# First layer of a three-layer token mixer: two projection tiles fed side by side, weight leads one tile ahead, one root a tile later

## What is computed

```python
def hybrid_layer(h, hc, c_act, cc_act, norm_g, w_mod, b_mod, w_in, ...):
    shift, scale, gate = jnp.split((c_act @ w_mod + b_mod)[:, None, :], 3, axis=-1)
    shift_c, scale_c, gate_c = jnp.split(cc_act @ w_mod + b_mod, 3, axis=-1)
    lat = split_cols((rms_norm(h, norm_g) * (1.0 + scale) + shift) @ w_in)
    cx = split_cols((rms_norm(hc, norm_g) * (1.0 + scale_c) + shift_c) @ w_in)
    att_l, att_c = gqa_branch(...)      # attention
    hg_l, hg_c = hgrn_branch(...)       # gated linear recurrence, per-head norm behind it
    y_conv, y_four, g_att, g_hg = mix_stream(lat, conv_w)   # convolution and Fourier mixing
    y = jnp.concatenate([y_conv, att_l * g_att, hg_l * g_hg, y_four], axis=-1) @ w_out
    h_new = h + gate * y
    ...

def first_block(...):
    for layer in range(DEPTH):          # DEPTH = 2
        h, hc = hybrid_layer(h, hc, ...)
    return rms_norm(h, final_g)
```

## Time and profile before

| | us |
|---|---|
| median of 3 runs | 1932.18 |
| lowest and highest | 1930.01, 1933.41 |
| the profiled execution | 1931.5 |
| its span | 1929.7 |
| TensorE busy | 1747.3 (91%) |
| VectorE busy | 824.2 (43%) |
| ScalarE busy | 716.7 (37%) |
| GpSimd busy | 601.3 (31%) |
| mean granted clock of TensorE, share of full | 0.963 |

### The profile page before, as it was taken

The page is one execution under the profiler, slowest core; times in us unless marked ns, Lnnn a source line. Parts: engine busy times, 40 slices in busy tenths (PEclk is TensorE's granted clock), DMA queues, the critical chain, the costliest instruction groups (busy, mean ns, idle before and its releaser), DMA issues.

```text
span 1929.7 us, 32336 instructions
## 1 busy us (share of the span) xinstructions
PE 1747.3 (91%) x13588; PEld 1403.6 (73%) x13588; DVE 824.2 (43%) x1489; ACT 716.7 (37%) x1111; POOL 601.3 (31%) x318
## 2 busy tenths in 40 slices
PE   6799899978989988889889988888899899999996
PEld 2687788855878766667777757886578588888885
DVE  0301165447250255476547658655415433333112
ACT  3323413235342624354543965003434432222222
POOL 0121312183223323452024303212234234444442
PEclk9899999989999999999899999899999999999998
DMA  8344311130122211302432210000220223323231
GB/s 329 106 155 142 112 35 46 46 109 1 55 90 74 66 56 56 131 1 95 135 99 87 77 44 2 3 3 22 66 85 25 66 78 97 98 90 97 98 109 66
DMA packets 42569, 152.17 MB, mean 79 GB/s; under 512 B 4416, under 2 KB 5568, under 8 KB 42176
## 3 DMA queue, kind: packets, MB, share of 16 engines
q1 hardware_dynamic: 38880, 140.72, 22.1%
q10 hardware_dynamic: 3552, 9.44, 1.3%
HBM read 145.95 MB, written 4.19 MB: 78 GB/s over the span
## 4 chain that ended last, share of the span: by engine, by line
PE 41%; DVE 7%; ACT 2%; issue 2%; DVEq 0%; ACTq 0%
PE wide_ps L1770 29%; PE wide_ps L1791 2%; PE pair_ps L2344 1%; PE wide_ps L2341 1%; PE wide_ps L2320 1%; PE wide_ps L2279 1%; DVE xn L1688 1%; DVE xn L1538 1%; PE duo_ps L2448 1%; PE wide_ps L2429 1%; DVE h L1692 1%; PE wide_ps L1806 1%; DVE ring_r L1182 1%; PE pair_ps L2279 0%; DVE work L1598 0%
## 5 line engine op out<-in xcount | busy, mean ns | idle before, releaser
L534 POOL TENSOR_TENSOR ring_r<-ring,scratch_r 128x1024 fp32r<-128x1024 f32 x179 | 433.1, 2420 | 1075.9 <-ACT scratch_r L706 1047.8
L1770 PE MATMUL wide_ps<-xn_r,scratch_r 128*128 128x512 f32 (+1 forms) x1320 | 490.1, 371 | 0.0
L1770 PE MATMUL wide_ps<-work_r,scratch_r 128*128 128x512 f32 (+1 forms) x1151 | 445.9, 387 | 23.3 <-DVE xn_r L1174 12.4
L706 ACT ACTIVATE scratch_r<-ring 128x1024 fp32r<-128x1024 f32 x195 | 206.7, 1061 | 599.8 <-PE wide_ps L1770 457.4
L1770 PE MATMUL wide_ps<-work_r,ring_r 128*128 128x512 f32 (+1 forms) x1151 | 429.2, 373 | 0.0
L1770 PEld LDWEIGHTS wide_ps<-xn_r,scratch_r 128*128 128x128 f32 x1320 | 252.1, 191 | 49.3 <-issue 5.7
L1770 PEld LDWEIGHTS wide_ps<-work_r,scratch_r 128*128 128x128 f32 x1151 | 218.7, 190 | 75.7 <-issue 19.1
L1770 PEld LDWEIGHTS wide_ps<-work_r,ring_r 128*128 128x128 f32 x1151 | 218.9, 190 | 40.0
L1770 PE MATMUL wide_ps<-proj_r,scratch_r 128*128 128x512 f32 x704 | 238.1, 386 | 1.6 <-DVE proj_r L1174 1.6
L1770 PEld LDWEIGHTS wide_ps<-proj_r,scratch_r 128*128 128x128 f32 x704 | 132.8, 189 | 31.6 <-DVE proj_r L1174 2.5
L693 ACT ACTIVATE proj<-wide_ps 128x512 f32<-128x512 f32 (+2 forms) x116 | 73.9, 637 | 164.4 <-PE wide_ps L1770 154.8
(11 more groups left out here) (406 smaller groups left out, 2913.6 us busy)
## 6 DMA issues: line engine op xcount, KB each, us to landing
ring<-weights SPq DMA_DIRECT2D x256, 512.0 KB, 3.5
h<-tokens SPq DMA_DIRECT2D x4, 768.0 KB, 11.6
h<-tokens ACTq DMA_DIRECT2D x1, 3072.0 KB, 10.2
out<-h ACTq DMA_DIRECT2D x1, 2048.0 KB, 7.3
h<-out ACTq DMA_DIRECT2D x1, 2048.0 KB, 10.7
out<-h SPq DMA_DIRECT2D x8, 256.0 KB, 2.0
const_sb<-const SPq DMA_DIRECT2D x1, 1089.0 KB, 6.1
h<-mem ACTq DMA_DIRECT2D x1, 1024.0 KB, 13.2
```

The source lines that it names most:

```text
L534: pool.tensor_tensor(as_r(wt), wt, as_r(w_lead(m)).bitcast(F32), ALU.subtract).then_inc(w_split, 1)
L706: act.activation(as_r(w_lead(m)), ring[:, c % RING, :], ACT.Copy).then_inc(w_lead_ready, 1)
L1770: last = pe.matmul(wide_ps[:, bank, a:b], wt[:, cols], as_r(x[:, a:b]), start=n == 0 and p == 0, stop=n == len(k_order) - 1 and p == 2)
```

## The change

In layer 0:

- The stream's order puts the four late chunks of tiles 0 and 1 first, and then the chunks of tiles 0 and 1.
- PE does the parts of both tiles, with the turn of the first row between them, and then `project_two` for tiles 0 and 1; tile 2 uses `project_ahead`. Both as layer 1 has it already.
- Leads 0 and 1 lie in spots of their own. ACT makes lead 0 before `modulate`, and lead 1 inside it, before k = 1, with a row copy before each; after that step t makes lead t + 1 (where it made t + 2), and step 15 makes 16 and 17.
- POOL waits at tile 2 for the last `x_split`, as in layer 1.

In both layers:

- For odd k ACT, not DVE, casts the lead of the input (`mod_lead`); DVE only subtracts.
- `head_root(ly, 0)` is asked for in ACT's step 24, where it was 23, so behind the evacuation of tile 23.

```diff
@@ -71,9 +71,9 @@
 
 
     if stage == "late":
-        return PLAN["proj0"] + 3 * (n // 2) + n % 2
+        return PLAN["proj0"] + (n if n < 4 else 3 * (n // 2) + n % 2)
     if stage == "proj0":
-        return PLAN["proj0"] + (3 * n + 2 if n < MIXED else 2 * MIXED + n)
+        return PLAN["proj0"] + (4 + n if n < 2 else 3 * n + 2 if n < MIXED else 2 * MIXED + n)
     return PLAN[stage] + n
 
 
@@ -236,6 +236,7 @@
         w_lead_ready, w_split = sem("w_lead_ready"), sem("w_split")
         lead_ready = sem("lead_ready")
         x_lead, x_split = sem("x_lead"), sem("x_split")
+        mod_lead = sem("mod_lead")
         norm_lead = sem("norm_lead")
         mix_split_lead, mix_split = sem("mix_split_lead"), sem("mix_split")
         final_ready = sem("final_ready")
@@ -324,7 +325,7 @@
                     conv_tmp[:, :], qe_2[:, :])[k]
 
 
-        LEAD_SPOTS = {SPLIT_AT[name] + n: (name, n) for name in ("proj1", "ab_2", "cq", "gu") for n in range(2)}
+        LEAD_SPOTS = {SPLIT_AT[name] + n: (name, n) for name in ("proj0", "proj1", "ab_2", "cq", "gu") for n in range(2)}
         X_SPLITS = {"proj0": 0, "out0": KT, "proj1": KT + 1, "out1": 2 * KT + 1, "ck": 2 * KT + 2, "ab_2": 3 * KT + 2,
                     "out_2": 4 * KT + 2, "cq": 4 * KT + 6, "gu": 5 * KT + 6, "down": 6 * KT + 6}
         MIX_ORDER = [0, 1, 4, 5, 6, 7, 2, 3]
@@ -352,7 +353,7 @@
 
             if m not in LEAD_SPOTS:
                 return scratch[:, CHUNK * (m % 2):CHUNK * (m % 2 + 1)]
-            spot_at = {"proj1": 4 * TOK, "ab_2": 22 * LAT + N_CONST2 + 2 * KT * CTX + 4 * LAT, "cq": 22 * LAT + N_CONST2 + 2 * KT * CTX,
+            spot_at = {"proj0": 4 * TOK, "proj1": 4 * TOK, "ab_2": 22 * LAT + N_CONST2 + 2 * KT * CTX + 4 * LAT, "cq": 22 * LAT + N_CONST2 + 2 * KT * CTX,
                        "gu": 22 * LAT + N_CONST2 + 2 * KT * CTX}[LEAD_SPOTS[m][0]] + CHUNK * LEAD_SPOTS[m][1]
             return flat[:, spot_at:spot_at + CHUNK]
 
@@ -528,7 +529,7 @@
                 for n in chunks or range(SPLIT_CHUNKS[stage]):
                     c, m = where(stage, n), SPLIT_AT[stage] + n
                     pool.wait_ge(w_lead_ready, m + 1)
-                    if n == 2 and stage in ("proj1", "cq", "gu"):
+                    if n == 2 and stage in ("proj0", "proj1", "cq", "gu"):
                         pool.wait_ge(x_split, X_SPLITS[stage] + KT)
                     wt = ring[:, c % RING, :]
                     pool.tensor_tensor(as_r(wt), wt, as_r(w_lead(m)).bitcast(F32), ALU.subtract).then_inc(w_split, 1)
@@ -719,10 +720,16 @@
 
                 act.wait_ge(mod_ready, (2, 4)[ly])
                 for k in range(KT):
+                    if ly == 0 and k == 1:
+                        modulation_row(KT + 1)
+                        weight_leads("proj0", 1)
                     act.wait_ge(scaled, 8 * ly + k + 1)
                     for s, (a, b) in enumerate(pieces(TOK)):
                         act.activation(xn_t[:, k, a:b], xn_t[:, k, a:b], ACT.Identity, bias=mod[:, ly, k, s:s + 1],
                                        scale=mod_scale[:, ly, k, s:s + 1]).then_inc(xn_ready, 1)
+                    if k % 2:
+                        act.wait_ge(xn_ready, 16 * ly + 2 * k + 2)
+                        act.activation(as_r(lead_tile(k)), xn_t[:, k, :], ACT.Copy).then_inc(mod_lead, 1)
 
             def lower_bounds():
 
@@ -802,7 +809,7 @@
                 if t == 22:
                     values_by_token(ly, 1)
                     head_square(ly, 0)
-                if t == 23:
+                if t == 24:
                     head_root(ly, 0)
                 if t == 25:
                     for d in range(2):
@@ -917,13 +924,16 @@
                         act.wait_ge(tokens_landed[k // 2], 16)
                         square(0, k, h[:, k, :], TOK)
                     mean_root(0, TOK)
-                    weight_leads("proj0", 0, 2)
+                    weight_leads("proj0", 0)
+                    modulation_row(KT)
                 modulate(ly)
                 for t in range(NPROJ):
-                    if ly == 0 and t < MIXED:
+                    if ly == 0 and 2 <= t < MIXED:
                         modulation_row(KT + t)
                     recurrent_steps(ly, t)
-                    if t < LATE:
+                    if ly == 0 and 1 <= t < LATE:
+                        weight_leads("proj0", t + 1, 2 if t == LATE - 1 else 1)
+                    elif ly and t < LATE:
                         leads_after(f"proj{ly}", t)
                     evacuate(f"proj{ly}", t, where(f"proj{ly}", t) + 1, width(ly, t), proj[:, t, 0:width(ly, t)],
                              other(ACT.Silu) if t in SILU_TILES else ACT.Copy, bank=None if t < LATE else 0)
@@ -1380,7 +1390,12 @@
                         dve.tensor_tensor(xn_t[:, k, :], h[:, k, :], root[:, :], ALU.mult).then_inc(scaled, 1)
                     if k:
                         dve.wait_ge(xn_ready, 16 * ly + 2 * k)
-                        split(xn_t[:, k - 1, :], lead_tile(k - 1))
+                        if k % 2:
+                            split(xn_t[:, k - 1, :], lead_tile(k - 1))
+                        else:
+                            dve.wait_ge(mod_lead, KT // 2 * ly + k // 2)
+                            dve.tensor_tensor(as_r(xn_t[:, k - 1, :]), xn_t[:, k - 1, :], as_r(lead_tile(k - 1)).bitcast(F32),
+                                              ALU.subtract).then_inc(x_split, 1)
                 queries_keys(ly)
                 dve.wait_ge(conv_out, 2 * ly)
                 link(dve.memset(proj[:, CV, :], 0.0))
@@ -1779,7 +1794,8 @@
                 banks = []
                 for stage, tile in (first, second):
                     g, m = EVAC[stage] + tile, SPLIT_AT[stage] + tile
-                    pe.wait_ge(evacuated, g - 1)
+                    if g >= 2:
+                        pe.wait_ge(evacuated, g - 1)
                     pe.wait_ge(w_split, m + 1)
                     banks.append((wide_ps[:, g % 2, :], as_r(w_lead(m)), as_r(ring[:, where(stage, tile) % RING, :])))
                 for k in range(KT):
@@ -2110,22 +2126,23 @@
             norm_step(0, KT - 1, TOK)
             for ly in range(DEPTH):
                 for t in range(NPROJ):
-                    if ly == 0 and 0 < t <= MIXED:
+                    if ly == 0 and 1 < t <= MIXED:
                         modulation_turn(KT + t - 1)
                     if ly == 0 and t == 0:
                         pe.wait_ge(mod_ready, 1)
                     if ly == 0 and t < MIXED:
+                        if t == 1:
+                            modulation_turn(KT)
                         for half in range(2):
                             modulation_part(MOD_BLOCKS[KT + t][0], 2 * MOD_BLOCKS[KT + t][1] + half)
                     query_key_sums(ly, t)
                     normed = lambda k: xn_t[:, k, :]
-                    if ly and t == 0:
-                        project_two(("proj1", 0), ("proj1", 1), lead_tile, normed, TOK, after(X_SPLITS["proj1"]))
-                    elif ly and t == 2:
-                        project_ahead("proj1", 2, lead_tile, normed, width(ly, 2))
-                    elif ly == 0 or t > 2:
-                        project_split(f"proj{ly}", t, range(KT), lead_tile, normed, width(ly, t),
-                                      after(X_SPLITS["proj0"]) if t == 0 else None,
+                    if t == 1:
+                        project_two((f"proj{ly}", 0), (f"proj{ly}", 1), lead_tile, normed, TOK, after(X_SPLITS[f"proj{ly}"]))
+                    elif t == 2:
+                        project_ahead(f"proj{ly}", 2, lead_tile, normed, width(ly, 2))
+                    elif t > 2:
+                        project_split(f"proj{ly}", t, range(KT), lead_tile, normed, width(ly, t), None,
                                       (lambda n: recurrent_piece(ly, KT * (t - LATE) + n)) if t >= LATE else None)
                 pe.wait_ge(hg_o, 2 * ly + 2)
                 fourier(ly)
@@ -2594,7 +2611,7 @@
         if ly == 0:
             late = np.concatenate([mods[1], mods[0][MOD_FIRST:]], 0).reshape(MIXED, 2, P, CHUNK)
             mixed = np.concatenate([late, proj[0:MIXED, None]], 1).reshape(3 * MIXED, P, CHUNK)
-            proj = np.concatenate([mixed, proj[MIXED:]], 0)
+            proj = np.concatenate([mixed[[0, 1, 3, 4, 2, 5]], mixed[6:], proj[MIXED:]], 0)
         stream += [proj, lat.astype(np.float32)]
         stream += [ctx.astype(np.float32)] if ly == 0 else []
         stream += [chunks_of(a["w_out"][ly][out_rows])]
```

## The result

| | before | after |
|---|---|---|
| median, us | 1931.1 (4 runs) | 1900.53 (4 runs) |
| lowest and highest | 1925.32, 1933.41 | 1899.6, 1902.04 |
| the profiled execution | 1931.5 | 1899.6 |
| its span | 1929.7 | 1897.8 |
| mean granted clock | 0.963 | 0.966 |

The account below looks back on a forecast made before the run. PE, busy 91% of the span, was taken as the bound. Gains of 6.9 (pair), 5.3 and 2.7 us (roots) sum to 14.9, taking 1931.5 to 1916.6; forecast median 1917 us, range 1912 to 1922.

Parts of the forecast that it names:

- the order on ACT: Layer 0, lead t+1 ahead of tile t's evacuation on ACT: no gain or cost, bound 0 to 2 us.
- leads one tile ahead come too late: Rival, `weight_leads` in tiles 2 to 14: ACT late beyond 1.44 us of slack, 13 times; 1939 us at 3.1 us; 4%.
- The start of the pair: Layer 0, tiles 0 and 1: starts at 54.05, ends at 73.9 instead of 80.84, gaining 6.9 us (5.8 to 10.4).
- hold the clock: Rival, start of layer 0: the parts' 1.5 us keep the grant, the pair costs 16.94 us, time 1914; 7%.
- the one with a late start: Rival, start of layer 0: the chain to the second weight tile adds 3 to 6 us, time 1920 to 1923; 7%.
- The way to 54 us: Before the pair: DVE's cast and subtraction run between POOL's two subtractions, 50.2 to 51.6, then POOL 51.6 to 54.0.
- The feed: Pair, odd casts on ACT: DVE about 4.1 us per two k against PE's 4.2, no wait added; layer 1 unchanged.
- The root in layer 0: `head_root` one tile later: 2.71 us of waiting and 2.9 us of low clock gone; 5.3 us gained (2.5 to 5.6).
- the rival in which DVE waits for the root: Rival, both roots: late root delays levels 4 and 5, part 2's 8.0 us are lost, time 1925; 12%.
- the other slack: Layer 0 root: DVE's 3.75 us wait for PE after level 3 shrinks to about one us, staying above nothing.
- The root in layer 1: `head_root` one tile later: 4.6 us gained less 1.9 of new waits for DVE, 2.7 us (0 to 4.6).

Follow-up runs that it names:

- D: The changed kernel with every cast of the input lead back on DVE, in both layers: 1902.36 us, ratio 0.9848.
- evac15_first: The changed kernel with the lead of tile 17 queued behind the evacuation of tile 15 on ACT, in both layers: 1898.27 us, ratio 0.983.

## Why the prediction was off, point by point

**The failed step: the order on ACT.** The sum put this term at nothing. The prediction wrote: "Evacuations come about 7 us earlier and nobody waits for them", and "Nothing for all of this, with 0 to 2 us as its bound." The first half was right and holds the whole gain. The second half had not been read off any row. Behind the evacuation stand the norm and the next row copy, and PE waits for that copy three times. The part gave 13.4 us by the rows (11.8 and 1.6), and its bound was 2. Two things in the reading led there. The prediction rests on PE's rows up to 81 us and again at the roots, and for the tiles between it takes the slack of tile 1, which "never waits"; but the norms begin at tile 8. And the edit was weighed only for the harm it could do, as in the rival with leads that come too late, never for a wait that stood there already. That rival, "leads one tile ahead come too late", falls: from 73.10 to 218.48 PE waits for nothing.

The rows at hand would have given the term. The earlier trace rows has the lead of tile 2 at 77.29, 6.35 us into the step that began at 70.94, after 8.87 us of waiting for the chunk. With the lead, the evacuation, 3.7 us for table load, Ln, Exp and square, and the row copy (1.06 + 0.8 + 3.7 + 0.4) that is 12.3 us for a step of 9.9: about 2.4 us of waiting, once for each of the three norms, and 2.7 us was known to bring the clock down. 3 x 2.4 + 2 or 3 x 1.7 is an estimate of 11 to 12 us.

**The start of the pair: right.** Foreseen 54.05, with 4.7 us of idle time before it and low clock to 60.0:

```profile
53.88 0.77 PE L1807 MATMUL wide_ps<-work_r,proj_r 128*128 128x512 f32 x1 [4.76 <-DVE xn_r L1184]
...
73.10 0.50 PE L1854 MATMUL duo_ps<-const_sb,proj 128*128 128x2 f32 x4
```

The clock was back at 58.8, so the low stretch is 4.9 us long and not 5.95, and costs 0.5 us less. The pair took 19.2 us for 19.9, without a wait. The two parts in the gap did not hold the clock (grant 0.68 over 46 to 54), and that rival falls, as does the one with a late start. The gain is 7.7 for 6.9. (One end of the range for the start was added wrongly: a lead that ends at 50.7 and a subtraction of 2.4 us give 53.1, not 53.4. The forecast does not hang on it.)

**The way to 54 us was another than the one written.** POOL and DVE between 47 and 54 us:

```profile
47.22 3.06 POOL L535 TENSOR_TENSOR ring_r<-ring,proj_r 128x1024 fp32r<-128x1024 f32 x1 [46.00 <-ACT proj_r L707]
...
50.57 2.35 POOL L535 TENSOR_TENSOR ring_r<-ring,proj_r 128x1024 fp32r<-128x1024 f32 x1 [0.30 <-ACT proj_r L707]
...
48.64 2.05 DVE L1182 CAST work_r<-xn 128x768 fp32r<-128x768 f32 x1 [0.58 <-ACT xn L728]
50.73 3.01 DVE L1184 TENSOR_TENSOR xn_r<-xn,work_r 128x768 fp32r<-128x768 f32 x1
```

I let DVE go between POOL's two subtractions. It was POOL that went on at once, at 50.57, in its usual 2.35 us, and DVE's subtraction took 3.01 us, where the same subtraction at 54.53 (L1397) takes 0.94; it ended 0.8 us behind POOL. That the start came out within 0.2 us of the 54.05 is luck, then: the order was the other one, and the chain of the two ends near 54 either way. The Trainium skill (SBUF — State Buffer, who interferes with whom) says that whichever starts first gets the shared pair for the whole instruction and the other blocks; here POOL started 0.16 us ahead and the trace agrees.

**The feed: right in time, idle as an edit.** No wait within the pair and nothing in layer 1, as foreseen; but D shows that DVE would have kept up alone.

**The root in layer 0: right.** 5.5 us for 5.3. The wait is gone and 318 to 332 us is all work at full clock. ACT and DVE there:

```profile
320.83 1.28 ACT L647 ACT_TABLE_LOAD   x1
322.12 0.90 ACT L657 ACTIVATE proj<-duo_ps,eps 128x768 f32<-128x768 f32 x1
323.06 0.85 ACT L658 ACTIVATE proj<-proj 128x768 f32<-128x768 f32 x1
...
321.36 2.33 DVE L1238 TENSOR_TENSOR h<-h 128x48 f32<-128x48 f32 x1
...
325.34 0.95 DVE L1278 TENSOR_TENSOR proj<-proj 128x768 f32<-128x768 f32 x1
...
327.27 0.62 DVE L1232 COPY_PREDICATED proj<-const_sb,wide_ps 128x192 f32<-128x192 int32 x2
```

The root is ready at 323.9, and DVE wants it at 325.34, after an operation of its own of 2.33 us beside POOL's (2.70 us from 320.89): it comes 1.4 us ahead of its use, and the rival in which DVE waits for the root falls. What was sized wrong is the other slack. The 3.75 us that DVE then waited for PE were to shrink to about one; the same row is now that of 327.27, and DVE does not wait at all there. PE still found everything ready, so it cost nothing, but the margin was thinner than foreseen. The Trainium skill (ScalarE: Activation LUTs, What ACT_TABLE_LOAD costs) adds a drain of 1.38 us to a load; here the lead before it ends at 320.81, the load begins at 320.83 and Ln follows at 322.12, so this trace shows 1.28 us and no drain.

**The root in layer 1: right, a little small.** 3.4 us for 2.7. The waits of PE for DVE are the ones expected, the new one (0.92) is smaller than the 1.4 us set for it, and the last (1.30, was 1.48 at 779.84) has not grown by the 0.5 us set for it:

```profile
729.15 0.67 PE L1927 MATMUL pair_ps<-h,proj 64*64 64x32 f32 x32 [1.50 <-DVE proj L1236]
...
739.21 0.67 PE L1927 MATMUL pair_ps<-h,proj 64*64 64x32 f32 x32 [0.92 <-DVE proj L1236]
...
748.41 0.77 PE L1883 MATMUL wide_ps<-const_sb,proj 128*128 128x128 f32 x5 [1.30 <-DVE proj L1236]
```

**Left open.** 1.5 us between tile 24 and layer 1, where the change edits nothing. It goes with the root: from the evacuation of tile 24 to layer 1's first it takes 218.0 or 218.1 us in all six kernels with the root in step 23, 216.4 to 216.7 us in five of the six with it in step 24, and 217.8 us in the sixth, evac15_first. Less of it runs at the lower clock: 380 to 420 us had a grant of 0.89 before, and 353 to 393 us one of 0.96 after. By what way the root's place decides that, and why not in evac15_first, was not tried.

## What to carry to other kernels

When an edit reorders an in-order queue, find the instruction in it that waits longest (here a lead in front of a chunk, 10.39 us), and follow everything behind it to the one that the busiest engine wants: what is cheap and ready must not stand behind what is waiting for a transfer. An edit that looks as if it could only hurt deserves the same search for waits of the bound engine over its whole stretch, with all of them listed, as an edit that is meant to help. Costs that repeat per step begin only where all parts of the step are present, so the first tiles are no sample for the later ones.
